# Adaptive modulation in a two-block transformer kernel: blocks 8 to 23 summed outside TensorE, and the constant tables loaded behind the input

## The reference, cut to what matters

```
s_lat, s_ctx = silu(c), silu(c_ctx)
mod   = s_lat @ ada_w + ada_b            # 2048 -> 12288
mod_c = s_ctx @ ada_w + ada_b
sh1, sc1, g1, sh2, sc2, g2 = split(mod, 6);   csh1, csc1, ... = split(mod_c, 6)
h  = modulate(rmsnorm(x, norm1_g), sh1, sc1)
hc = modulate(rmsnorm(ctx, norm1_g), csh1, csc1)
... x = x + g1 * mixed;  x = x + g2 * mlp(modulate(rmsnorm(x, norm2_g), sh2, sc2))
```

## Time and profile before

| | |
|---|---|
| median of 3 runs | 3230.01 us (3219.39 to 3234.2) |
| the profiled execution's own time | 3229.23 us |
| span of the profile | 3227.4 us |
| PE busy, weight loads busy | 3089.8 us (96%), 2696.5 us (84%) |
| DVE, ACT, POOL busy | 1917.2, 1415.5, 244.4 us |
| bytes read | 608.12 MB, 191 GB/s over the span |

### The profile page before, as it was taken

One profiled execution on the slowest core, in us unless ns is written; L12 is line 12 of the kernel. 1 busy time (PEld: TensorE's weight loads), 2 busy tenths in 40 slices (PEclk: granted clock), 3 DMA queues, 4 the chain that ended last, 5 costly groups with the idle time before them and its releaser, 6 DMA issues.

```text
span 3227.4 us, 54438 instructions
## 1 busy us (share of the span) xinstructions
PE 3089.8 (96%) x22670; PEld 2696.5 (84%) x22670; DVE 1917.2 (59%) x2598; ACT 1415.5 (44%) x1994; POOL 244.4 (8%) x203
## 2 busy tenths in 40 slices
PE   7999989899999999999999999999998999999998
PEld 6898978787888888888788889988877888888887
DVE  5475763543755785555555565345667666666666
ACT  4343442433544573444434454343425445444443
POOL 1100321020100110000000230010001000000002
PEclk9999999999999999999999999999999999999999
DMA  6554555546644666777777777763434566656654
GB/s 213 177 159 132 156 177 198 189 157 207 228 153 148 205 191 191 230 253 241 256 246 253 249 242 239 252 187 115 159 104 147 173 205 182 187 180 194 187 177 146
DMA packets 535783, 620.07 MB, mean 192 GB/s; under 512 B 19451, under 2 KB 459926, under 8 KB 534177
## 3 DMA queue, kind: packets, MB, share of 16 engines
q1 hardware_dynamic: 527008, 586.51, 57.7%
q0 software_dynamic: 3344, 23.78, 2.1%
q10 hardware_dynamic: 5184, 6.29, 0.6%
HBM read 608.12 MB, written 8.39 MB: 191 GB/s over the span
## 4 chain that ended last, share of the span: by engine, by line
PE 78%; DVE 4%; ACT 2%; DMA 2%; issue 1%; POOL 0%; SPq 0%; ACTq 0%; DVEq 0%; POOLq 0%
PE psum L591 35%; PE psum L592 18%; PE psum L563 3%; PE psum L566 3%; PE psum L565 3%; PE psum L691 3%; PE psum L1749 2%; PE psum L625 2%; PE psum L627 2%; PE psum L628 2%; DVE wlo L520 1%; DMA wraw<-in_ffn_w 1%; PE psum L675 1%; PE psum L2398 0%; PE psum L1940 0%
## 5 line engine op out<-in xcount | busy, mean ns | idle before, releaser
L513 ACT ACTIVATE whi<-wraw 128x1024 fp32r<-128x1024 f32 (+1 forms) x948 | 977.7, 1033 | 1203.7 <-PE psum L592 455.4
L520 DVE TENSOR_TENSOR wlo<-wraw,whi 128x1024 fp32r<-128x1024 f32 (+1 forms) x948 | 1150.8, 1226 | 559.6 <-ACT whi L513 552.6
L591 PE MATMUL psum<-g,whi 128*128 128x512 f32 x2816 | 1000.9, 397 | 15.8 <-issue 8.2
L591 PE MATMUL psum<-h,whi 128*128 128x512 f32 x2240 | 793.4, 396 | 5.0 <-DVE h L2037 2.4
L592 PE MATMUL psum<-g,wlo 128*128 128x256 f32 x2816 | 788.3, 280 | 0.0
L591 PEld LDWEIGHTS psum<-g,whi 128*128 128x128 f32 x2816 | 530.5, 188 | 162.9 <-issue 25.9
L592 PE MATMUL psum<-h,wlo 128*128 128x256 f32 x2240 | 633.6, 283 | 0.0
L592 PEld LDWEIGHTS psum<-g,wlo 128*128 128x128 f32 x2816 | 530.7, 188 | 0.5
L591 PEld LDWEIGHTS psum<-h,whi 128*128 128x128 f32 x2240 | 421.2, 188 | 122.9 <-issue 21.9
L592 PEld LDWEIGHTS psum<-h,wlo 128*128 128x128 f32 x2240 | 421.7, 188 | 0.2
L563 PE MATMUL psum<-h,whi 128*128 128x256 f32 x1040 | 304.3, 293 | 35.1 <-DVE h L896 22.0
(11 more groups left out here) (468 smaller groups left out, 3368.2 us busy)
## 6 DMA issues: line engine op xcount, KB each, us to landing
wraw<-in_ffn_w SPq DMA_DIRECT2D x256, 512.0 KB, 6.7
wraw<-in_w_in SPq DMA_DIRECT2D x204, 512.0 KB, 4.7
wraw<-in_ada_w SPq DMA_DIRECT2D x192, 512.0 KB, 4.8
wraw<-in_ffn_w_up SPq DMA_DIRECT2D x160, 512.0 KB, 4.5
wraw<-in_w_out SPq DMA_DIRECT2D x64, 512.0 KB, 4.5
wraw<-in_ffn_w_down SPq DMA_DIRECT2D x64, 512.0 KB, 4.6
wraw<-in_xattn_wk SPq DMA_DIRECT2D x32, 512.0 KB, 4.5
wraw<-in_xattn_wv SPq DMA_DIRECT2D x32, 512.0 KB, 4.6
```

Source lines behind the costliest of these rows:

```text
L513: e.activation(high(i), view(WRAW[i % NR], i), ACT.Copy).then_inc(*hi.up(i))
L520: e.tensor_tensor(low(i), view(WRAW[i % NR], i), high(i).bitcast(F32), SUB).then_inc(*lo.up(i))
L591: e.matmul(both_of(g, j), w_hi[:, kk, s:s + 128], X[:, k, :], start=k == 0, stop=False, skip_group_check=True)
```

## The change

Blocks 8 to 23 are no longer multiplied by TensorE. For each of them one engine scales every k-row of the weights by its own `silu(c)` value (one per partition) and adds the 16 rows up in a 128 x 2 x 512 accumulator (`ACM`, in the place of the context tile `CX`); its two halves are added, and TensorE only sums over the partitions with a matmul against ones (`gather_p`, 8 instructions as before). Who sums: VectorE for blocks 8, 9, 12, 13, 16, 17, 20, 21 (`rows_v`); for the blocks in `BY_POOL` ScalarE scales in place in `WRAW` (`times_a`) and GpSimd adds (`rows_g`).

The chunks now come one at a time behind every second main chunk. `ada2` is blocks 8 to 21, beside `dn0`, `up1`, `dn1`, ..., `up3`, `dn3`, two blocks to a product, so that VectorE's blocks fall on the `dn` products and the shared ones on the `up` products; `ada3` is blocks 22 and 23, beside `k2x` and `v2x`, both shared. `weave` in `xk` and `xv` keeps its two chunks at a time.

At the start `MT` is asked for on ScalarE's queue behind `x`, GpSimd's filter loads wait until the last part of `x` has landed, and TensorE's and VectorE's waits for `MT` move into the side work.

```diff
-WF = 4
+WF = 2
-WC = 4
+WC = 2
-NA2 = 20
+BY_POOL = (10, 11, 14, 15, 18, 19, 22, 23)
...
+                    if n >= NA0:
+                        summed[len(chunks) - 1] = ada.v if n not in BY_POOL else ada.g if k else ada.a
...
-        woven = plan_ada("ada2", NA0, NA2)
+        woven = plan_ada("ada2", NA0, 22)
...
-            made(weave(plan(f"dn{i}", "ffn_w2", 16 * i, 16, cols(0, 2048, 256), "v"), woven if i else iter(()), WF))
-        woven = plan_ada("ada3", NA2, 24)
+            made(weave(plan(f"dn{i}", "ffn_w2", 16 * i, 16, cols(0, 2048, 256), "v"), woven, WF))
+        woven = plan_ada("ada3", 22, 24)
...
+        def rows_v(e, n, ci, ids, acc):
+            a, (i, k0, m), before = acc[:, n % 2, :, :], ids[ci], ids[ci - 1][0]
...
+            for kk in range(2):
+                w, by = view(WRAW[i % NR], i)[:, kk, :], SF[:, k0 + kk, 0:1]
+                if ci == 0:
+                    x = e.tensor_scalar(a[:, kk, :], w, by, None, MUL)
+                else:
+                    x = e.scalar_tensor_tensor(a[:, kk, :], w, by, a[:, kk, :], MUL, ADD)
+            x.then_inc(*ada.v.up(("sum", i)))
+            if ci == 7:
+                e.wait_ge(*ada.v.now())
+                e.tensor_tensor(a[:, 0, :], a[:, 0, :], a[:, 1, :], ADD).then_inc(*ada.v.up(("acc", n)))
+
+        def times_a(e, n, ci, ids, acc):
+            i, k0, m = ids[ci]
...
+            landed(e, i)
+            for kk in range(2):
+                w = view(WRAW[i % NR], i)[:, kk, :]
+                x = e.activation(w if ci else acc[:, n % 2, kk, :], w, ACT.Copy, scale=SF[:, k0 + kk, 0:1])
+            x.then_inc(*ada.a.up(("times", i)))
+
+        def rows_g(e, n, ci, ids, acc):
+            a, (i, k0, m) = acc[:, n % 2, :, :], ids[ci]
+            e.wait_ge(*ada.a.at("times", i))
+            if ci:
+                if ci > 1:
+                    e.wait_ge(*ada.g.now())
+                e.tensor_tensor(a, a, view(WRAW[i % NR], i), ADD).then_inc(*ada.g.up(("sum", i)))
+            if ci == 7:
+                e.wait_ge(*ada.g.now())
+                e.tensor_tensor(a[:, 0, :], a[:, 0, :], a[:, 1, :], ADD).then_inc(*ada.g.up(("acc", n)))
...
+        def gather_p(e, n, acc):
+            e.wait_ge(*(ada.g if n in BY_POOL else ada.v).at("acc", n))
+            for j in range(4):
+                x = e.matmul(PSUM[:, ada_bank(n), 2 * j:2 * j + 2], acc[:, n % 2, 0, 128 * j:128 * j + 128], ones[:, 0:2], start=True, stop=True)
+            x.then_inc(*ada.p.up(("mod", n)))
...
+        def mod_a(e, name, acc, hi_to, weight=None):
+            for n, ids in PL[name]:
+                for ci, (i, k0, m) in enumerate(ids):
+                    hi_to(e, reach(i, 3))
+                    if n in BY_POOL:
+                        times_a(e, n, ci, ids, acc)
+                    yield weight
...
         def sync(e):
             e.dma_start(PK[:, :], A_["pack"]).then_inc(*d_pk.up("all"))
-            e.dma_start(MT[:, :], A_["mats"]).then_inc(*d_mt.up("all"))
             for i in range(len(chunks)):
                 j = i - NR
-                if j in plain:
+                if j in summed:
+                    e.wait_ge(*summed[j].at("times" if summed[j] is ada.a else "sum", j))
+                elif j in plain:
                     e.wait_ge(*mm.at("chunk", j))
...
         def gpsimd(e):
             ada_first_g(e)
+            e.wait_ge(*d_x0[3].at("all"))
             load_filters(e)
```

More of the change, by code:

```diff
@@ L159, in part, with weave @@
         yield next(steps)
-def weave(main, extra, per):
+def weave(main, extra, per, times=1):
     n = 0
@@ L168, in weave @@
         if n % per == 0:
-            for other in islice(extra, 2):
+            for other in islice(extra, times):
                 yield other
@@ new lines, in mod_v, with mod_g @@
+        def mod_v(e, name, acc, lo_to, weight=None):
+            for n, ids in PL[name]:
+                for ci, (i, k0, m) in enumerate(ids):
+                    lo_to(e, reach(i, 2))
+                    if ci == 6 and n > NA0:
+                        modulation_v(e, n - 1)
+                    if n not in BY_POOL:
+                        rows_v(e, n, ci, ids, acc)
+                    yield weight
+        def mod_g(e, name, acc):
+            for n, ids in PL[name]:
+                for ci in range(8):
+                    if n in BY_POOL:
+                        rows_g(e, n, ci, ids, acc)
@@ new lines, in gather_p, with mod_p @@
+        def gather_p(e, n, acc):
[3 more added lines that the diff above has]
+            x.then_inc(*ada.p.up(("mod", n)))
+        def mod_p(e, name, acc, weight=None):
+            for n, ids in PL[name]:
+                for ci in range(8):
+                    if ci == 2 and n > NA0:
+                        gather_p(e, n - 1, acc)
+                    yield weight
@@ L2503, in tensor @@
         def tensor(e):
-            e.wait_ge(*d_mt.at("all"))
-            side = Side(sums_p(e, fn, TM1, False, 0.3), idle(1), spectrum_p(e))
+            side = Side(then(lambda e: e.wait_ge(*d_mt.at("all")), e), sums_p(e, fn, TM1, False, 0.3), idle(1), spectrum_p(e))
             side.beside(gemm_p(e, PL["in_ssd"], [(HH, HL)], lambda e, k: e.wait_ge(*fn.v.at("lo", k // 4))), RSPEC)
@@ L2679, in vector @@
             made(extra)
-            side = Side()
+            side = Side(idle(5), then(lambda e: modulation_v(e, 23), e))
             for b in range(2):
@@ L2732, in scalar @@
                 x_high(e, g)
-            side = Side(sums_a(e, fn, X0, TM1, RS1[:, :], None, 0.3), then(fn.ended, e), spectrum_a(e))
+            side = Side(idle(1), sums_a(e, fn, X0, TM1, RS1[:, :], None, 0.3), then(fn.ended, e), spectrum_a(e))
             side.beside(stream(e, hi_to, 3, PL["in_ssd"], None, gate_a), RSPEC)
@@ L2745, in scalar @@
             extra = ada_a(e, "ada1", MO0[:, :], hi_to, WA)
-            side.beside(weave(stream(e, hi_to, 3, PL["xk"], None, xk_store_a), extra, WK), RW)
+            side.beside(weave(stream(e, hi_to, 3, PL["xk"], None, xk_store_a), extra, WK, 2), RW)
             xk_store_a(e, 14)
             xk_store_a(e, 15)
-            side.beside(weave(tok_stream(e, hi_to, 3, PL["xv"], 2, xv_evac_a, lambda e, ci: ci and mix_a(e, ci - 1)), extra, WV), RW)
+            side.beside(weave(tok_stream(e, hi_to, 3, PL["xv"], 2, xv_evac_a, lambda e, ci: ci and mix_a(e, ci - 1)), extra, WV, 2), RW)
             made(extra)
```

90 lines of the change are left out of this document (47 added, 43 removed).

## The result

The changed kernel takes 3462.43 us (median of 4 runs, 3460.31 to 3467.44) beside 3230.27 for the kernel before (4 runs, 3219.39 to 3234.2): a ratio of 1.0727, with an interval of 1.0698 to 1.0755. That is 232 us slower, where +177 was forecast: the direction and the range hold, the sum is 55 us short.

The account below looks back on a forecast made before the run. TensorE, 96% busy, was taken as the bound, with the ring replacing it in shared blocks: -76.2 + 291 - 20 - 9 - 0.9 - 8 = +177 us on 3229.23, so 3406 us; range 3315 to 3495.

Parts of the forecast that it names:

- The mechanism: Shared blocks: landing, split, times_a, GpSimd's add and SP's next issue run in series, so the ring becomes the bound, +291 us.
- TensorE's 76 us: Sixteen blocks' modulation matmuls (L691) taken off TensorE: 16 x 4 groups x 1.19 us, -76.2 us.
- Rival 1: TensorE stays the bound, modulation buffers coming back within its pace: 3144 us, chance 0.10.
- The trip: Shared blocks, one buffer from issue to issue per three chunks: 10.2 us where TensorE needs 5.6.
- the credit: Entries to the four shared stretches: TensorE's chunks already split ahead take back 5 us each, -20 us.
- rival 2: VectorE's ring trip doesn't fit either, up to 12.4 us for 11.2: +38, 3444 us, chance 0.09.
- The start: First weight chunk lands sooner without filters and MT ahead; TensorE starts at 14 instead of 22.02: -8 us.
- The clock: Shared trips: TensorE's slower work at a lower granted clock mostly swallowed by gaps; taken as 0, at worst +64 us.
- Rival 4: TensorE's lower clock costs time after all: +30 to 64 us, 3436 to 3470 us, chance 0.08.
- high bound: Shared trip with GpSimd's add at 3.4, times_a 1.3, landing 5.3: 11.2 us, whole change +240 us.
- rival 3: GpSimd's adds take 3.4 us under VectorE's splits: 56 x 0.8 = +45, 3451 us, chance 0.12.
- rival 5: Shorter shared trips, 8.5 to 9.4 us: 3300 to 3330 us, chance 0.06.

Follow-up runs that it names:

- experiment 1: Changed kernel, but ScalarE splits two main chunks ahead instead of three in up1 to up3, k2x and v2x: 3182.38 us.
- experiment 5: Changed kernel, but ScalarE scales each shared modulation chunk (times_a) at its own place in the walk, still splitting three ahead: 3151.09 us.
- experiment 3: Changed kernel without GpSimd's 56 adds, the buffer given back by times_a: 3299.16 us.
- experiment 8: Changed kernel with blocks 8 to 19, 22 and 23 in the shared form, 48 more trips: 3677.38 us.
- experiment 6: Changed kernel with times_a and also VectorE's rows_v at each chunk's own place in the walk: 3146.55 us.
- experiment 7: Changed kernel with VectorE summing all sixteen blocks, each chunk at its own place in the walk: 3144.76 us.
- experiment 2: Changed kernel with BY_POOL empty, VectorE summing all sixteen blocks, ScalarE still splitting three ahead: 3198.36 us.
- experiment 4: Kernel before the change with only the new start (MT behind x, filter loads after x): 3220.67 us, ratio 0.9973.

## Why the prediction was right, and where its sum was off

**The mechanism is shown.** ScalarE does stand behind the landing of i+4, GpSimd behind ScalarE, SP behind GpSimd, all in one chain with no overlap. Experiments 1 and 5 change only the order and win 280 and 311 us; 3 and 8 change the length of the trips or their number, and the time follows. Nearly all errors of the sum have one sign, so the range wasn't met by errors that cancel.

**TensorE's 76 us** are real and were hidden by the ring: experiments 5 to 7 bring them out (80, 85 and 86 us below the kernel before, some 9 of them the start's). Rival 1's 3144 is what the mended order gives. As a statement on this change it was wrong. By the rule of the Trainium skill (Perfetto Trace Analysis, Identifying the Most-Contended Engine) the busiest engine is the one to optimize first. TensorE was that (its weight loads, which the page goes by, were busy 84%, VectorE 59%), and relieving it made the kernel 232 us slower; the traces agree with the rule only in experiments 1, 2 and 5 to 7, where the moved work holds up the ring little or not at all.

**The trip.** Taken 10.2, and with the post steps 10.3 on average over an `up` product; measured 10.65 in `up1` and 10.50 to 10.65 in `k2x` and `v2x` (SP's issues at 2227.78, 2238.28, 2248.93). The term that was mis-sized is the landing: 5.2 taken, 5.7 measured in the mean of `up1`'s sixteen trips (5.5 to 6.4, from SP's issue of the modulation chunk to the landing of the second chunk of the burst, the one that ScalarE waits for), and 5.7 in the median of `k2x` and `v2x`. The others come to -0.2 together: `times_a` 1.32 against 1.2 (two of 707 ns; the plain copy of the earlier trace rows was a little cheap for an activation with a scale per partition), the add 2.43 in the mean against 2.6, from landing to `times_a` 0.99 without and 1.74 with the post step against 1.05 and 1.9, semaphores 0.11 against 0.15. I took the landing from bursts of six with two modulation chunks at their head; the second of a burst landed 5.2 us after the first issue there (median of 49 bursts) and lands 5.7 after it in a burst of three. That was not foreseen, and why stays open. The trip's error makes 5.6 us per `up` product, 17 in all, of the 55.

**The step that failed: what the stretch gives back.** I credited 5 us at each entry and 9 for gathers, 29 us in all. The table shows what happened instead. The `up` products alone cost +56.8, +60.6 and +59.1, as forecast with the credit. But each `dn` product, which should have been 9.5 us shorter, was 2 to 12 longer. The lead moves the waits and saves nothing: TensorE's long waits begin 33 us into `up1`, and the last one, 8.46 us, ends 14 us into `dn1`, since SP issues the first main chunks of `dn1` behind the last modulation chunks of `up1`. Waits of TensorE in `dn1` (in total, times, longest):

```profile
PE psum L592 <- DVE wlo L521: 9.4, 4, 8.5
PE psum L592 <- DVE h L2118: 0.7, 1, 0.7
```

These 10.1 us eat the 9.5 that the removed L691 should give. Of the 2.8 us that are left of `dn1`'s +3.4, the pairs at the lower clock level behind that wait (3.7 us at half the pace) make 1.8; the last one stays open. Without the credit and gathers, a pair comes to 49 + 5 + 2 + 5.6 = 61.6, and `up1` with `dn1` measured 60.2, `up2` with `dn2` 62.6. That the credit fails is read from the trace and this sum; no run took the lead away, and the sum can't tell the gathers' 2 us from nothing.

**dn3 costs more: +71.0 for the pair.** Here GpSimd sums the squares of the residual beside VectorE, and VectorE's two L746 take longer: 1030 ns each, 746 in `dn1`. Of the 28 in `dn3`, the 17 that start while GpSimd works take 1.22 us in the mean, the other 11 take 0.74, as all do in `dn1`, where GpSimd does nothing. First line `dn3`, second `dn1` (group, count, busy us and mean ns, idle before):

```profile
L746 DVE SCALAR_TENSOR_TENSOR cx<-wraw,sf,cx 128x512 f32<-128x512 f32 x28 | 27.7, 1030 | 0.0
...
L746 DVE SCALAR_TENSOR_TENSOR cx<-wraw,sf,cx 128x512 f32<-128x512 f32 x28 | 19.7, 746 | 0.0
```

TensorE's waits from `dn3`'s start to 2110 us; the 9.4 us among the first row's are the last wait of `up3`'s stretch:

```profile
PE psum L592 <- DVE wlo L521: 11.6, 6, 9.4
PE psum L564 <- DVE xt L1945: 5.5, 1, 5.5
```

VectorE falls behind, and at the end TensorE waits 5.5 us for the last `XT` tiles, which it did not before. That is rival 2 in small, in one product out of four. In `dn0` nothing was added (+0.9 for the stage with `up0`), as forecast. That the instructions are longer beside GpSimd is shown; that the 9 us over the other pairs all come from it is an argument from these rows, and no run separated it.

**Behind block 23** I took another 0.9 us off, for a wait of TensorE that would go. Instead it waited 8.68 us for GpSimd's last sum:

```profile
2342.35 1.86 PE L792 MATMUL psum<-mats,cx 128*128 128x2 f32 x8 [8.68 <-POOL cx L771]
```

GpSimd's last two adds still came 10.1 and 8.5 us behind the one before, and its sum of the halves took 2.13, while TensorE, having begun `q2`, stood at the gather, its next instruction in order. That `k2c` to the final layer is only 8 us above the forecast must come from a larger lead: SP issued block 22's first chunk 17.1 us ahead of `k2x`'s first matmul (2163.46, 2180.57), where `up1` had 1.7 (1284.28, 1285.97). This is a reading of the trace; no run separated it.

**The start** gave 5.2 us at `up0` in this kernel and 5 to 12 in experiment 4, for the 8 forecast; the first matmul came at 13.97, as computed (14).

**The clock.** Taken as 0, with +64 at worst. TensorE's granted clock was 0.81 in the shared stretches and its work there took longer (102.64 us busy for 492 matmuls, which at `dn0`'s pace of 915 in 160 us need 86). At that pace its work would fill 54% of the window, the 55% of the forecast, and not 64%. The longer work lay in time that was idle anyway: the `up` products cost what the trips alone give. Rival 4 is out but for what it adds at the exits.

Together: trips +17 and +5 (`k2x`, `v2x`, 0.3 each), entries and gathers of the three pairs +21, `dn3` +9, the last gather +10, less what is left over there and put down to the larger lead (-8), start +3, `dn0` +1, the end -4: 54 of the 55.

**Two slips in the prediction** don't change its sum. L864 and L1364 are not the same add: L1364 multiplies two other tensors, so its 3.407 us are no price of an add, and as a sign of the locked port pair the two rows prove nothing (the last section has rows that do). The high bound and rival 3 rest on that figure; the 56 adds took 2.34 to 2.63 us. And the two ends of rival 5 go by different terms: a trip of 8.5 gives 3300 with the post steps, one of 9.4 gives 3330 only without them and 3355 with them.

## What to carry to other kernels

Before work is moved off the busiest engine, follow one buffer of the ring from issue to issue and add up every step that an in-order engine puts between having the data and giving it back; shares of busy time don't show that. An engine that waits for a later landing before it gives back a buffer that it already has turns the ring's depth into latency: in experiment 5 buffers are given back in the order in which they landed, and the same engines fit. A lead at the entry to a starved stretch was no credit where another product followed; it only moved the wait.

## What the runs showed of the hardware

A VectorE instruction with two inputs in SBUF that meets a GpSimd add is held until the add ends, and then does its own work. VectorE's step of 128x256 (L2095), 0.43 us when alone, took 1.95 beside the add of 1322.36 and ended 0.28 us behind it; a subtraction of 1.22 (L521) took 2.72 beside the one of 1334.30 and ended 1.08 us behind it:

```profile
1322.36 2.35 POOL L768 TENSOR_TENSOR cx<-cx,wraw 128x1024 f32<-128x1024 f32 x1 [7.92 <-ACT wraw L759]
1334.30 2.54 POOL L768 TENSOR_TENSOR cx<-cx,wraw 128x1024 f32<-128x1024 f32 x1 [9.60 <-ACT wraw L759]
```

```profile
1323.04 1.95 DVE L2095 SCALAR_TENSOR_TENSOR rb<-rb,rs 128x256 f32<-128x256 f32 x1
1325.36 0.43 DVE L2095 SCALAR_TENSOR_TENSOR rb<-rb,rs 128x256 f32<-128x256 f32 x1
...
1335.20 2.72 DVE L521 TENSOR_TENSOR wlo<-wraw,whi 128x1024 fp32r<-128x1024 f32 x1 [0.61 <-ACT whi L514]
```

An instruction that reads one input from PSUM (L2091, 0.42 us) is not held: 24 of them start inside an add of the changed kernel, and all take 0.42 to 0.43. It goes the other way, too: where an add starts while an L521 has 0.29 to 0.36 us left, the L521 keeps its 1.22 and the add takes 2.54 to 2.63 (18 of them), where the other 38 take 2.34 to 2.41. In experiment 5, where they meet more often, single adds take up to 3.48. The Trainium skill (SBUF — State Buffer, SBUF: two separate sides) states that whichever of the two starts first has the shared port pair for its whole instruction and the other waits; these rows agree in both directions.

The second chunk of a burst lands 5.06 to 6.02 us after its own issue in `up1` after the change (median 5.3) and 4.8 to 5.2 in experiment 3 (median 5.1), whose bursts are made of the same three chunks. What makes the difference stays open.
